# Ten of the 62 tap products of a 31-tap depthwise convolution, taken from TensorE and given to VectorE

## What is computed

```python
def conformer_conv(u, dw_w, dw_b, ln_g, ln_b, pw_w):
    a, b = jnp.split(u, 2, axis=-1)
    h = a * jax.nn.sigmoid(b)
    h = causal_depthwise_conv(h, dw_w) + dw_b.astype(h.dtype)
    h = layer_norm(h, ln_g, ln_b)
    h = jax.nn.silu(h)
    return h @ pw_w.astype(h.dtype)
```

## Time and profile before

| | |
|---|---|
| median of three runs | 1060.62 us (1060.6 to 1062.25) |
| the profiled execution's own time | 1060.3 us |
| its span, first to last instruction | 1058.5 us |
| PE busy | 1050.9 us, 99% |
| DVE busy | 864.5 us, 82% |
| ACT busy | 685.4 us, 65% |
| POOL busy | 346.4 us, 33% |
| the convolution branch on PE | 789.28 to 804 us of the span |

### The profile page before, as it was taken

How to read it: one execution, slowest core, us unless ns; L and a number is a source line. 1 busy time by engine, 2 the same in 40 slices (tenths; PEclk the granted TensorE clock), 3 DMA queues, 4 the chain that set the end, 5 groups by cost and what they waited for, 6 DMA issues and landing times.

```text
span 1058.5 us, 21199 instructions
## 1 busy us (share of the span) xinstructions
PE 1050.9 (99%) x7503; PEld 976.4 (92%) x7503; DVE 864.5 (82%) x1584; ACT 685.4 (65%) x1257; POOL 346.4 (33%) x373
## 2 busy tenths in 40 slices
PE   8999999999999999999999999999999999999998
PEld 7999999999999999999989899999998998999998
DVE  7777778777799888887776999888896769998886
ACT  6766767766766555576776766555685767665553
POOL 5222222112355333332121564333350015533331
PEclk9999999999999999999999999999999999999999
DMA  8644454456466555435453566555434436655541
GB/s 295 225 161 154 150 180 155 149 170 210 148 216 217 196 181 193 166 103 178 153 180 121 198 208 202 187 187 190 146 106 149 141 120 203 216 197 185 192 157 41
DMA packets 57989, 183.33 MB, mean 173 GB/s; under 512 B 6464, under 2 KB 10048, under 8 KB 57664
## 3 DMA queue, kind: packets, MB, share of 16 engines
q1 hardware_dynamic: 57056, 181.51, 52.1%
q10 hardware_dynamic: 864, 0.92, 0.3%
HBM read 181.35 MB, written 1.05 MB: 172 GB/s over the span
## 4 chain that ended last, share of the span: by engine, by line
PE 96%; DVE 1%; POOL 1%; DMA 1%; issue 0%; ACT 0%; SPq 0%; DVEq 0%; POOLq 0%
PE ps L408 23%; PE ps L410 12%; PE ps L648 9%; PE ps L650 9%; PE ps L649 9%; PE ps L1702 6%; PE ps L1704 6%; PE ps L1703 6%; PE ps L1187 2%; PE ps L1188 2%; PE ps L1189 2%; PE ps L807 1%; PE ps L852 1%; PE ps L781 1%; PE ps L819 1%; PE ps L838 1%
## 5 line engine op out<-in xcount | busy, mean ns | idle before, releaser
L369 DVE TENSOR_TENSOR w_lo<-w_raw,w_hi 128x1024 fp32r<-128x1024 f32 (+2 forms) x371 | 446.0, 1217 | 51.3 <-ACT w_hi L361 50.9
L361 ACT ACTIVATE w_hi<-w_raw 128x1024 fp32r<-128x1024 f32 (+2 forms) x371 | 355.4, 972 | 156.4 <-PE ps L410 130.4
L408 PE MATMUL ps<-xg,w_hi 128*128 128x512 f32 x1056 | 370.4, 395 | 0.0
L410 PE MATMUL ps<-xg,w_lo 128*128 128x256 f32 x1056 | 292.7, 277 | 0.0
L408 PEld LDWEIGHTS ps<-xg,w_hi 128*128 128x128 f32 x1056 | 198.0, 188 | 44.0
L410 PEld LDWEIGHTS ps<-xg,w_lo 128*128 128x128 f32 x1056 | 198.3, 188 | 0.1
L648 PE MATMUL ps<-w_hi,xg 128*128 128x384 f32 (+1 forms) x560 | 194.2, 347 | 1.4 <-DVE w_lo L369 1.4
L1824 POOL TENSOR_TENSOR prob_t<-prob_t,qkT 128x256 f32<-128x256 f32 x63 | 101.2, 1607 | 284.8 <-ACT prob_t L1747 284.8
L650 PE MATMUL ps<-w_hi,xg 128*128 128x384 f32 (+1 forms) x560 | 187.8, 335 | 0.0
L649 PE MATMUL ps<-w_lo,xg 128*128 128x384 f32 (+1 forms) x560 | 187.5, 335 | 0.0
L1702 PE MATMUL ps<-g_hi,w_hi 128*128 128x256 f32 x528 | 148.2, 281 | 0.1
(11 more groups left out here) (181 smaller groups left out, 1387.6 us busy)
## 6 DMA issues: line engine op xcount, KB each, us to landing
w_raw<-w_stream SPq DMA_DIRECT2D x228, 512.0 KB, 3.7
w_raw<-w_stream SPq DMA_DIRECT2D x139, 384.0 KB, 3.4
w_raw<-w_stream SPq DMA_DIRECT2D x4, 392.0 KB, 2.9
con<-consts SPq DMA_DIRECT2D x1, 1024.0 KB, 7.7
xT<-x_t SPq DMA_DIRECT2D x4, 256.0 KB, 5.0
conv_taps<-taps SPq DMA_DIRECT2D x1, 1024.0 KB, 7.7
xT<-x_a SPq DMA_DIRECT2D x3, 256.0 KB, 6.7
par<-params SPq DMA_DIRECT2D x1, 592.0 KB, 4.6
```

Of the source, the lines that this page charges most:

```text
L361: nc.scalar.activation(w_hi[s][:, 0:w], w_raw[s][:, 0:w], ACT.Copy).then_inc(w_hi_done, 1)
L369: nc.vector.tensor_tensor(w_lo[s][:, 0:w], w_raw[s][:, 0:w], w_hi[s][:, 0:w].bitcast(F32), ALU.subtract).then_inc(w_lo_done, 1)
L408: nc.tensor.matmul(bank(b, 0, 2 * TOK), w_hi[s][:, k * P:(k + 1) * P], xg[:, k, :, :].rearrange("p h t -> p (h t)"), start=(k == 0), stop= ...
L410: last = nc.tensor.matmul(bank(b), w_lo[s][:, k * P:(k + 1) * P], xg_hi[:, k, :], start=False, stop=(k == KT - 1), skip_group_check=True)
```

## The change

`STEPS_PE` gives PE seven steps for tile 0 and six for tile 1 in place of eight, so 28 and 24 matmuls of the 32 and 32. The taps that these left out (28 to 30 of tile 0, 24 to 30 of tile 1) are computed by the new `conv_taps_dve` from `cv_h[t]`. It runs in DVE's step n = 0 behind the shift copies (tile 0) and in step n = 2 behind `conv_out_dve(0)` (tile 1). Each of its instructions waits for the one before. The bias goes into its first instruction; `conv_out_dve` adds PE's sums to the result. The parameter load grows by 14 columns.

```diff
+STEPS_PE = (7, 6)
+TAP0 = SHIFTS * min(STEPS_PE)
...
-N_PAR = PAR_PW + 2 * 2 * P
+PAR_TAP = PAR_PW + 2 * 2 * P
+N_PAR = PAR_TAP + 2 * (CONV_C - TAP0)
...
             if n == 0:
                 conv_shift_dve(eng, 1, 1)
+                conv_taps_dve(eng, 0)
             if n == 2:
                 conv_out_dve(eng, 0)
+                conv_taps_dve(eng, 1)
             if n == 3:
                 conv_out_dve(eng, 1)
...
-        for m in range(STEPS):
+        for m in range(STEPS_PE[t]):
...
+    def conv_taps_dve(eng, t):
+
+        eng.wait_ge(pre_dve, t + 1)
+        eng.wait_ge(rest_in, 32)
+        for j in range(SHIFTS * STEPS_PE[t], CONV_C):
+            n = conv_tap_no(t, j)
+            w = par[:, PAR_TAP + 2 * (j - TAP0) + t:PAR_TAP + 2 * (j - TAP0) + t + 1]
+            if j == SHIFTS * STEPS_PE[t]:
+                nc.vector.tensor_scalar(cv_acc[t], cv_h[t][:, j:j + TOK], w, par[:, PAR_DWB + t:PAR_DWB + t + 1],
+                                        ALU.mult, ALU.add).then_inc(conv_tap, 1)
+            else:
+                eng.wait_ge(conv_tap, n)
+                nc.vector.scalar_tensor_tensor(cv_acc[t], cv_h[t][:, j:j + TOK], w, cv_acc[t],
+                                               ALU.mult, ALU.add).then_inc(conv_tap, 1)
+
+    def conv_tap_no(t, j):
+
+        return t * (CONV_C - SHIFTS * STEPS_PE[0]) + j - SHIFTS * STEPS_PE[t]
+
     def conv_out_dve(eng, t):
         eng.wait_ge(conv_done, t + 1)
-        nc.vector.tensor_scalar(cv_acc[t], bank(CONV_BANK + t), par[:, PAR_DWB + t:PAR_DWB + t + 1], None,
-                                ALU.add).then_inc(conv_acc, 1)
+        eng.wait_ge(conv_tap, conv_tap_no(t, CONV_C))
+        nc.vector.tensor_tensor(cv_acc[t], bank(CONV_BANK + t), cv_acc[t], ALU.add).then_inc(conv_acc, 1)
```

More of the change, by code:

```diff
@@ L330, in build @@
     conv_acc = sem("conv_acc")
+    conv_tap = sem("conv_tap")
     ln_sq = sem("ln_sq")
@@ L1954, in conv_pe @@
                 last = nc.tensor.matmul(bank(CONV_BANK + t)[c * BLOCK:(c + 1) * BLOCK, :], taps[:, w:w + BLOCK],
-                                        cv_shift[t][c][:, SHIFTS * m:SHIFTS * m + TOK], start=(m == 0), stop=(m == STEPS - 1),
+                                        cv_shift[t][c][:, SHIFTS * m:SHIFTS * m + TOK], start=(m == 0), stop=(m == STEPS_PE[t] - 1),
                                         skip_group_check=True)
         last.then_inc(conv_done, 1)
+    def conv_taps_dve(eng, t):
[13 more added lines that the diff above has]
+        return t * (CONV_C - SHIFTS * STEPS_PE[0]) + j - SHIFTS * STEPS_PE[t]
     def conv_out_dve(eng, t):
         eng.wait_ge(conv_done, t + 1)
-        nc.vector.tensor_scalar(cv_acc[t], bank(CONV_BANK + t), par[:, PAR_DWB + t:PAR_DWB + t + 1], None,
-                                ALU.add).then_inc(conv_acc, 1)
+        eng.wait_ge(conv_tap, conv_tap_no(t, CONV_C))
+        nc.vector.tensor_tensor(cv_acc[t], bank(CONV_BANK + t), cv_acc[t], ALU.add).then_inc(conv_acc, 1)
         if t == 1:
@@ L2296, in parameters @@
     cols(PAR_PSC, w["pool_scale_2"][0])
+    for j in range(TAP0, CONV_C):
+        cols(PAR_TAP + 2 * (j - TAP0), w["conv_dw_w_2"][0][j])
     par[:, PAR_BF:PAR_BF + HEADS_C] = w["b_f_2"][0]
```

## The result

The changed kernel takes 1065.94 us (median of 6 runs, 1064.32 to 1066.66), the kernel before 1060.82 beside it (6 runs). The ratio is 1.0035, 95% interval 1.0025 to 1.0046: 2.7 to 4.9 us slower. The forecast was 1061.4, no measurable change, 1059.4 to 1063.2. It was wrong.

What follows compares the result with a forecast made beforehand. PE was taken to bound the kernel, busy 99%. Saving -1.29, new wait +1.55 at L1969 and +0.48 at L1984 gave +0.75 us, added to the 1060.62 median: forecast 1061.4 us, range 1059.4 to 1063.2.

Steps and rivals of the forecast that it cites:

- What bounds the kernel, and where the slack is: Whole kernel and stage three: PE bounds, busy 99%; DVE has 1.16 us slack ahead of L1969, none ahead of L1984.
- PE saves 1.29 us: Convolution in stage three: dropped matmul steps save 0.43 us for tile 0 and 0.86 for tile 1.
- Price of the products: DVE's tap products: 0.515 us per scalar_tensor_tensor, 0.35 for the first; tile 0 taken at 1.85 us, tile 1 at 3.48.
- Rule on two SBUF sources: DVE's eight new scalar_tensor_tensors: the skill page's half throughput would about double each and give 1065.2 us; prediction preferred the rows.
- Rival 2: DVE's tap products: scalar_tensor_tensors at double length, 3.8 us in front of L1965, giving 1065.2 us; chance 0.08.
- A new wait of 1.55 us at the sum, and 0.75 us late at the variance: Stage three: PE waits 1.55 us for DVE at L1969, then passes L1984 0.75 us later, with 0.48 more wait.
- Rival 1: Stage three: DVE is done in time and PE keeps its 1.29 us gain, giving 1059.3 us; chance 0.09.
- rival 3: Chunk 4 behind the new wait at L1969: PE's clock falls to 1.2 GHz, giving 1063.6 us; chance 0.03.
- Nothing given back later: Behind L1984: PE has no further wait in the stage to catch up in, so +0.75 us stays to the end.
- rival 4: Later than L1984: the delay grows because DVE or ACT is still behind at PE's next chunk, up to 1063.4; chance 0.05.
- Edits at nothing: Later splits, SP's loads behind them and the parameter load's extra 7 KB: all taken as covered, costing nothing.

Runs made afterwards that it cites:

- TensorE's part alone: Kernel before with 28 and 24 of the 32 and 32 tap matmuls and no products on VectorE: 1061.14 against 1062.36 us, ratio 0.9988.
- the run with the own tile for the tap weights: Changed kernel with its 14 columns in a separate tile behind all others, other tiles as in the kernel before: 1062.88 against that kernel's 1062.36 us, ratio 1.0003.
- VectorE's part alone: Changed kernel with tap weights in their own tile, ten products on VectorE, all 64 matmuls kept on TensorE: 1063.04 against 1062.36 us for the kernel before.
- the new order: Changed kernel, tap weights in their own tile, VectorE's products, sums and centring moved ahead of splits: 1059.58 against 1062.36 us for the kernel before.

## Why the prediction was wrong, point by point

- *What bounds the kernel, and where the slack is*: right. With PE's work unchanged, the products on DVE use up the 1.16 us, PE waits 0.17 us at the sum (0.27 by the forecast), and what is late behind it shows at the variance in full.
- *PE saves 1.29 us*: right, 1.29 by the stretch of the run with TensorE's part alone.
- *Price of the products*: right. Six take 3.09 us for 3.09 forecast, the tensor_scalar 0.40 (0.35 taken, 0.478 the other end). Beside POOL tile 0's three took 2.5 us (793.89 to the end at 796.40), above my upper bound of 2.0; the two splits behind them took 1.81 instead of 2.25, because POOL was done at 796.12. The two errors cancelled, which is luck: `conv_out_dve(0)` starts at 798.07, less the 2.27 us of lateness 795.80; forecast 795.7.
- *Rule on two SBUF sources*: by the Trainium skill ("Vector Engine (DVE) Microarchitecture Reference", "Points that are easy to get wrong") the estimate was 0.94 us for each; without POOL beside them the rows say 0.515 from start to start. Rival 2 fell. Its 1065.2 us lie near the measured 1065.94 by chance.
- *A new wait of 1.55 us at the sum, and 0.75 us late at the variance*: 1.47 and 0.78. The wait at the variance is 0.53 us, where over 0.7 was to show the mechanism: PE also comes later to it. L1965's end at 803.59 is past the 803 that was to mean rival 2, but only because all of stage three starts 2.27 us late; without that it is 801.3, as forecast. Rival 1 fell, and rival 3 too: the granted clock stays at 1.00 through the wait and behind it.
- *Nothing given back later*: right as far as stage three goes. From its first tap matmul to the first down projection behind it PE takes 97.76 us before, 98.71 in the changed kernel and 98.56 with every tile in its old place: 0.8 to 0.95 more, so rival 4 fell too.
- *"Edits at nothing: ... The load of parameters grows by 14 columns"*: **here it failed.** I costed the transfer and not the tile. The wider tile moves all tiles behind it, and that is some 3 of the 3.7 us: 32 bytes alone gave +3.5, and the change without the displacement +0.3 (+0.5 among executions of like clock). The distances of start to start that show it lie in the feed-forward stages, which the list of edits never reached. No case of the prediction had this mechanism, and the range was too narrow by a term that was missing, not by one that was mis-sized.

The changed kernel is then 0.8 (stage three) + 2.8 to 3.5 (place) = 3.6 to 4.3, with 2.7 to 4.9 measured and +4.0 between the two profiled spans.

## What to carry to other kernels

A change that widens a tile is two changes: check what it does to the start of every tile behind it, and keep the starts when the edit itself is to be measured. Where PE is the bound, try a few displacements of the tiles it streams; here 32 bytes cost 2 to 3.5 us, 192 cost 7 and 128 gained 6.5, more than any edit of the work in stage three. And where executions differ in a way that has nothing to do with the edit, compare like with like: the 0.5 us of the change without its displacement show only so. Last, idle time of an engine can be filled for nothing only if what stands behind it in the queue is not waited for: the same ten products on VectorE made stage three 0.8 us longer than before in the first order, and 1.4 shorter in the other.

## What the runs showed of the hardware that was not expected

**The pace of float32 matmuls depends on where the streamed tile lies against the tiles ahead of it in SBUF.** 24 matmuls of 256 columns took 2623 to 2761 ns on average at six distances; everything moved together changed the time by -0.4 us, which its interval does not tell from nothing. The Trainium skill's page "SBUF — State Buffer" ("SBUF: two separate sides") says of the engines' side that only the pair of ports shared by VectorE and GpSimd causes contention and that PE never waits. These runs do not show which two accesses meet, but PE's pace with the same instructions was not constant; the measurement decides. That the partner is the weight tile is argued, from the worst case at equal places modulo 256 and the best at 64 bytes short of it, and was not tried by moving the weights alone. Why an up projection slows when g_hi moves stays open, and so does why a stage of the old distances has two paces.

**PE's clock can fall behind the wait for the first row sums.** In 6 of the 18 profiled executions, the wait of some 1.4 us that ends near 24 us is followed by a stretch at the lower of the two levels. The windows view of the run with the own tile for the tap weights, against that of TensorE's part alone:

```profile
22.00:24.00 2.00, 0.59 (x6) 0.50 (x5) 2.00 (x2) 0.00 (x0) 1.92 (x3) 1.00 0.86 260
24.00:28.00 4.00, 4.00 (x16) 4.00 (x17) 3.37 (x7) 3.06 (x9) 4.00 (x12) 0.57 0.94 297
```

```profile
22.00:24.00 2.00, 0.87 (x8) 0.78 (x6) 2.00 (x3) 0.00 (x0) 1.92 (x2) 1.00 0.91 295
24.00:28.00 4.00, 3.69 (x23) 3.69 (x24) 3.42 (x6) 2.99 (x9) 4.00 (x11) 1.00 0.87 272
```

16 matmul starts in place of 23 within 4 us, at a mean granted clock of 0.57: an estimated 4 x (1 - 0.57) = 1.7 us, if PE were bound throughout. The two traces differ by less. The first down projection starts at 298.67 and 297.48, 1.2 us apart. The first feed-forward stage, in its slower pace, adds 0.6, and stage three begins 1.5 us later in the one than in the other (791.08 and 789.56). The Trainium skill ("TensorE: Matmul & The Clock Gate", "HAM oscillation — how this bites in real kernels") tells of such falls behind waits, in a kernel whose waits are longer. The six traces show one behind a wait of 1.4 us, and the twelve others, with the same wait, that it need not happen. The wait of 1.5 us at the sum over channels never had one in the four profiles that contain it. For rival 3 of the prediction I had read one execution, in which the clock held; its row was no proof that it always does.

The six profiled executions with the fall have a mean granted clock of 0.998 and the twelve others 1.00, and all but two of the unprofiled ones have one of the two (or 0.999, counted as 1.00). The executions of the kernel before with 0.998 are on average 1.2 to 1.7 us slower than those with 1.00, in each of the four measurements that list both, which is much of their scatter. The fall comes long before the convolution, so executions of one mean clock can be compared with each other. In us against before (95%), among them: the change with every tile in its old place +0.5 (0.3 to 0.8), TensorE's part alone -1.1 (-1.4 to -0.9), VectorE's part alone +0.7 (0.4 to 0.9), the new order -1.5 (-1.7 to -1.3), 32 bytes behind the parameters +3.2 (3.0 to 3.4).
